# First mixer, weight units 10 to 36: the low part formed by an accumulating transfer (raw added to minus high) instead of by VectorE's subtraction

## The reference

```
def first_block(x, mem, ...):
    h = rmsnorm(x, norm_mix_g[i])
    c_q, c_kv, k_r, u_ssm, x_q, gate_logits = split_combined(h @ w_in[i])
    y_a = mla_branch(c_q, c_kv, k_r, ...) @ w_o_mla[i]       # causal attention, 8 heads
    y_b = s5_branch(u_ssm, ...) @ w_o_ssm[i]                 # complex linear scan over the tokens
    y_c = cross_branch(x_q, mem, ...) @ w_o_cross[i]         # attention to 256 memory rows
    gates = jax.nn.sigmoid(gate_logits + b_gate[i]).reshape(bsz, l, N_BRANCH, D_MODEL)
    merged = gates[:, :, 0] * y_a + gates[:, :, 1] * y_b + gates[:, :, 2] * y_c
    x = x + merged @ w_out[i]
    ...                                                      # feed-forward part with a convolution
```

## Time and profile before

| | |
|---|---|
| median of 3 runs | 1732.19 us (1731.37 to 1732.69) |
| span of the profiled execution | 1730.6 us |
| PE busy | 95% of the span |
| DVE busy | 62% |
| ACT busy | 42% |
| POOL busy | 11% |
| data moved by DMA | 284.23 MB, 164 GB/s in the mean |

### The profile page before, as it was taken

The page is one execution under the profiler, slowest core; times in us unless marked ns, Lnnn a source line. Parts: engine busy times, 40 slices in busy tenths (PEclk is TensorE's granted clock), DMA queues, the critical chain, the costliest instruction groups (busy, mean ns, idle before and its releaser), DMA issues.

```text
span 1730.6 us, 28437 instructions
## 1 busy us (share of the span) xinstructions
PE 1639.9 (95%) x11368; PEld 1516.5 (88%) x11368; DVE 1080.5 (62%) x1271; ACT 731.1 (42%) x771; POOL 198.5 (11%) x188
## 2 busy tenths in 40 slices
PE   6888788989999999999999999989999999999998
PEld 5876677889998999988998999989998999989997
DVE  6779996777777555555456655555555555665555
ACT  6344225454545333345434433343333553443332
POOL 4935570000000000001000000000000020000000
PEclk9989899999999999999999999989999999999999
DMA  6412323355553554544344554545554444545552
GB/s 243 147 73 98 107 95 140 124 210 187 190 188 127 195 195 177 187 151 166 147 170 146 199 195 173 191 148 174 191 188 151 186 153 149 174 180 186 182 191 97
DMA packets 39613, 284.23 MB, mean 164 GB/s; under 512 B 4513, under 2 KB 4513, under 8 KB 5729
## 3 DMA queue, kind: packets, MB, share of 16 engines
q1 hardware_dynamic: 38864, 278.93, 44.6%
q0 software_dynamic: 384, 2.98, 0.5%
q10 hardware_dynamic: 272, 1.05, 0.2%
HBM read 281.89 MB, written 1.05 MB: 163 GB/s over the span
## 4 chain that ended last, share of the span: by engine, by line
PE 82%; DVE 9%; POOL 4%; issue 3%; ACT 2%; DMA 0%; DVEq 0%; ACTq 0%; POOLq 0%
PE p L614 19%; PE p L615 19%; PE p L616 19%; PE big L614 7%; PE big L615 7%; PE big L616 7%; DVE ar L1523 2%; DVE wlo L510 2%; DVE ar L1784 1%; POOL sm L525 1%; POOL ar L544 1%; ACT whi L502 1%; DVE ar L1531 1%; POOL ar L548 0%; PE p L786 0%
## 5 line engine op out<-in xcount | busy, mean ns | idle before, releaser
L510 DVE TENSOR_TENSOR wlo<-raw,whi 128x2048 fp32r<-128x2048 f32 x256 | 591.3, 2312 | 338.8 <-ACT whi L502 337.2
L614 PE MATMUL p<-h_hi,whi 128*128 128x256 f32 x2568 | 735.1, 286 | 6.8 <-DVE h_lo L1531 5.9
L615 PE MATMUL p<-h_lo,whi 128*128 128x256 f32 x2568 | 731.0, 285 | 0.0
L616 PE MATMUL p<-h_hi,wlo 128*128 128x256 f32 x2568 | 730.6, 285 | 0.0
L502 ACT ACTIVATE whi<-raw 128x2048 fp32r<-128x2048 f32 x256 | 488.9, 1914 | 320.1 <-PE big L616 163.7
L614 PEld LDWEIGHTS p<-h_hi,whi 128*128 128x128 f32 x2568 | 497.4, 194 | 18.2 <-issue 9.2
L615 PEld LDWEIGHTS p<-h_lo,whi 128*128 128x128 f32 x2568 | 497.5, 194 | 1.8
L616 PEld LDWEIGHTS p<-h_hi,wlo 128*128 128x128 f32 x2568 | 497.1, 194 | 0.0
L614 PE MATMUL big<-whi,b_hi 128*128 128x512 f32 x454 | 177.9, 392 | 1.0 <-DVE b_lo L1523 1.0
L615 PE MATMUL big<-wlo,b_hi 128*128 128x512 f32 x454 | 177.5, 391 | 0.0
L616 PE MATMUL big<-whi,b_lo 128*128 128x512 f32 x454 | 176.6, 389 | 0.0
(11 more groups left out here) (238 smaller groups left out, 1606.9 us busy)
## 6 DMA issues: line engine op xcount, KB each, us to landing
raw<-weights SPq DMA_DIRECT2D x263, 1024.0 KB, 4.8
ar<-consts POOLq DMA_DIRECT2D x1, 2112.0 KB, 8.3
ar<-mem ACTq DMA_DIRECT2D x1, 1024.0 KB, 6.6
x_rows<-x SPq DMA_DIRECT2D x1, 1024.0 KB, 10.2
out<-ar SPq DMA_DIRECT2D x2, 512.0 KB, 2.7
ar<-ssm_bc SPq DMA_DIRECT2D x1, 512.0 KB, 14.7
ar<-g_final POOLq DMA_DIRECT2D x1, 512.0 KB, 4.0
c<-consts SPq DMA_DIRECT2D x1, 504.5 KB, 4.2
```

The source lines that it names most:

```text
L510: dve.tensor_tensor(wlo[:, r, :], raw[:, r, :], whi[:, r, :].bitcast(F32), ALU.subtract)\
L614: pe.matmul(out, s[0], m[0], start=start, stop=False)
L615: pe.matmul(out, s[0], m[1], start=False, stop=False)
L616: return pe.matmul(out, s[1], m[0], start=False, stop=stop)
```

## The change

For units 10 to 36 DVE's subtraction is gone. ACT writes `wlo` too, right behind `whi`, as the raw weights rounded in the same way and negated (so minus high). POOL then issues a transfer that reads the unit from memory once more and adds it to `wlo` in place. The PE waits for that transfer's own semaphore, one per slot of the ring (`lo_in0` to `lo_in2`). SP's load of the next raw unit waits for `split_done`, which ACT counts up for these units when minus high is written, and DVE for all others.

```
+LO_BY_DMA = range(10, U_MIX1)
...
-                    sp.wait_ge(S("lo_done"), i * RING + (r + 1))
+                    sp.wait_ge(S("split_done"), i * RING + (r + 1))
                     sp.dma_start(raw[:, r, :], ws[i * RING + (RING + r)]).then_inc(S(f"raw_in{r}"), 16)
...
             act.activation(whi[:, r, :], raw[:, r, :], ACT.Copy).then_inc(S("hi_done"), 1)
+            if l is None and us in LO_BY_DMA:
+                if us == LO_BY_DMA[0]:
+
+                    act.wait_ge(S("split_done"), us)
+                act.activation(wlo[:, r, :], raw[:, r, :], ACT.Copy, scale=-1.0).then_inc(S("split_done"), 1)
 
         def split_dve(dve, s, l=None, m=None):
-            r = (ustat(s, l) + RING) % RING
+            us = ustat(s, l) + RING
+            if l is None and us in LO_BY_DMA:
+                return
+            r = us % RING
...
+            def add_raw(u):
+
+                r = u % RING
+                pool.wait_ge(S("split_done"), u + 1)
+                nc.gpsimd.dma_start(wlo[:, r, :], ws[u], accum_op=ALU.add).then_inc(S(f"lo_in{r}"), 16)
+
...
             for j in range(ST):
                 rotate_out(j)
+                add_raw(j + 10)
                 if j == 3:
                     rsqrt(rc, msc, 4, "big_read", plan.use("cs") + 1, "c_rstd")
                 if j == 11:
                     rsqrt(rq_, mq, 16, "mq_msq", 1, "mq_rstd")
                     rsqrt(rk_, mk, 16, "mk_msq", 1, "mk_rstd")
+            for u in range(ST + 10, U_MIX1):
+                add_raw(u)
             norm(2)
...
             def unit_in(k, l=None, extra=0):
 
-                pe.wait_ge(S("lo_done"), extra + unit(k, l) + 1)
+                if l is None and k in LO_BY_DMA:
+                    pe.wait_ge(S(f"lo_in{k % RING}"), 16 * len(range(LO_BY_DMA[0] + (k - LO_BY_DMA[0]) % RING, k + 1, RING)))
+                    return
+                pe.wait_ge(S("split_done"), extra + unit(k, l) + 1)
```

More of the change, by code:

```diff
@@ L477, in _ @@
                 for r in range(RING):
-                    sp.wait_ge(S("lo_done"), i * RING + (r + 1))
+                    sp.wait_ge(S("split_done"), i * RING + (r + 1))
                     sp.dma_start(raw[:, r, :], ws[i * RING + (RING + r)]).then_inc(S(f"raw_in{r}"), 16)
             for u in range(RING + turns * RING, U_ALL):
-                sp.wait_ge(S("lo_done"), u - RING + 1)
+                sp.wait_ge(S("split_done"), u - RING + 1)
                 sp.dma_start(raw[:, u % RING, :], ws[u]).then_inc(S(f"raw_in{u % RING}"), 16)
@@ L510, in split_dve @@
             dve.tensor_tensor(wlo[:, r, :], raw[:, r, :], whi[:, r, :].bitcast(F32), ALU.subtract)\
-               .then_inc(S("lo_done"), 1)
+               .then_inc(S("split_done"), 1)
         @block.gpsimd
@@ L1730, in first_split @@
                 dve.wait_ge(S("hi_done"), r + 1)
-                low(wlo[:, r, :], raw[:, r, :], whi[:, r, :]).then_inc(S("lo_done"), 1)
+                low(wlo[:, r, :], raw[:, r, :], whi[:, r, :]).then_inc(S("split_done"), 1)
             dve.wait_ge(S("mem_in"), 16)
```

## The result

| | before | after |
|---|---|---|
| median of 4 runs | 1732.1 us (1731.37 to 1732.69) | 1761.8 us (1755.35 to 1768.15) |
| recorded ratio | | 1.0168, 95% interval 1.0152 to 1.0184 |
| span of the profiled execution | 1730.6 us | 1753.7 us |
| mean granted clock of it | 0.976 | 0.971 |

The change makes the kernel slower by 29.7 us in the median.

The account below looks back on a forecast made before the run. DVE was taken to bound the scan's stretch. With +28.5 us there and +9 in the tail, +37.5 on 1732.2 gave 1770 us; the forecast's own range was 1750 to 1795, the wider one 1735 to 1860.

Parts of the forecast that it names:

- L: Time from a transfer's issue on POOL to its landing, taken as 8.1 us; bounds 4.8 and 11.4.
- The path S + R + L: Scan: from unit j + 8's start to unit j + 10's takes at least one PE slot, the rotation and the transfer's landing.
- The steps: Units 10 to 24: seven steps of two slots, 148.0 us against 145.5 before; with the added terms +28.5 us.
- Clock, +12: Scan's stretch: the PE's 4.5 us wait in each of seven steps lowers its clock, losing 1.7 us each time.
- Rotation, 7 x 4.4: Scan's stretch: each of seven steps includes a POOL rotation of 4.4 us before the transfer.
- Sharing, +10: Scan's stretch: raw loads beside the adds share the DMA engines, 1.5 us for each step; bounds 0 and 23 in all.
- Instructions behind rotation 11, +3: On POOL, two instructions of 6.9 us delay rotation 12 and its transfer; 3.6 us of slot cover the rest.
- The tail, +9: Units 25 to 36: +7 for the longer way through ACT and transfer, +3 for the clock, -1 for the attention's chain.
- ACT's pass: 27 more passes on ACT of 1.91 us each, 17 of them fitting in the scan's stretch.
- One pass: Rival: the add costs nothing beside copying, landing in 4.8 us; about -16 us, 1716 us; chance 0.08 for 1710 to 1728.
- covered: Rival: landing takes 5.5 to 7 us and waits are too short to lower the clock; 1735 to 1752 us, chance 0.13.
- dearer: Rival: the add costs more than two passes, 11.4 us giving 1803 us; chance 0.20 for 1795 to 1860, 0.05 beyond.

Follow-up runs that it names:

- Plain: The changed kernel with its transfer as a plain load overwriting `wlo` with the raw weights instead of adding to it: 1728.8 us, ratio 0.9973 to the kernel before.
- no_add_scan: Against the changed kernel, units 10 to 25 have no transfer, ACT writing scaled raw weights as low part; later units keep DVE's subtraction: 1710.4 us, ratio 0.9877.

## Why the prediction was right, and where its sizes were off

The forecast was 1770 us, the result 1761.8: the side, the mechanism and the likeliest case are right. The forecast loss of 37.5 us was 7.8 too high in the median and 14.4 against the profiled execution.

**L, right.** Taken as 8.1 us, measured 8.6 in the median and 7.9 to 8.7 for the seven transfers on the chain between 99 and 275 us. Plain fits an L made of two passes, as assumed: about 2.3 us fixed and twice 2.8, for my 1.5 and twice 3.3. The Trainium skill's rule for a ReduceScatter ("Collectives: The Full Stack", section "The bandwidth ceiling: the fold count and why AG ≠ RS ≠ AR"), an add costs its two source reads at half the rate, agrees with this: 5.4 against 2.8 us of the engines' time for each unit. The Trainium skill's line for this queue ("DMA: Bandwidth & Descriptors", section "Anatomy of one DMA — SWDGE (gpsimd) path"), 2.0 us plus bytes over 436 GB/s, gives 4.4 us for the plain unit and 6.8 for the added one as an estimate; the shortest measured are 5.1 and 7.9.

**The path S + R + L, right.** Units 12, 14, 16, 18, 20, 22 and 24 each started within 0.1 us after their transfer had landed. The chain of the profile first runs through the same path of the odd units (13, 15, 17) and from unit 18 on through 20, 22 and 24. From 13 to 18 the PE waited for a transfer at every unit, and then at every second, as forecast. The step from unit 10 to 12 ran over DVE and an attention product, which ended with the transfer. The rotations are released by L819, and placing the transfer ahead of the rotation (early) takes the path away and 33 us with it.

**The steps.** From unit 10 by pairs to unit 24 the working, with its clock, sharing and the instructions behind rotation 11, gives 30.7, 23.2, 21.8, 23.7, 23.7, 26.7 and 23.7, together 173.5 us. Measured: 30.3, 22.2, 21.8, 22.3, 23.5, 23.9, 23.5, together 167.4. That is 22 us more than before, where 28 were forecast, and the unit-10 start was 0.7 us earlier rather than 1 later. The terms inside it are less right than their sum, which is luck in part: the clock cost more than forecast, the sharing nothing.

- *Clock, +12: too small.* The seven slots, from the start of unit 10, 12 and so on to the rotation that each slot's output releases, took 17.2, 9.6, 9.1, 9.7, 10.7, 10.8 and 10.8 us, together 78.0, where the sum had 60.5 at full clock. The PE was busy in nearly all of it, at mean clocks of 0.70 to 0.82 (10.8 us at 0.72 is 7.8 at full clock), so some 17 us were lost, in the last three slots 2.7 to 2.9 each where I had put 1.7. (The 9.3 us above are less because the kernel before lost time to the clock too.)
- *Rotation, 7 x 4.4: nearly right.* From a rotation's start to the issue behind it 4.5 to 4.7 us went by, 1.8 us more in all, as the 0.3 us between the two were not in the sum.
- *Sharing, +10: the step that failed.* I let each transfer on the path take 1.5 us longer for the raw load beside it. The transfers on the chain took 7.9 to 8.7 us, 8.2 in the mean, so 0.1 where 1.5 was put. It is not that the raw loads stayed away. Beside the transfer of unit 18 one was issued 2.2 us ahead of it and landed 2.7 us after its issue, and the DMA engines were busy all the time (share 1.06), yet it landed in 7.9 us:

```profile
196.00:203.80 7.80, 4.04 (x25) 2.81 (x23) 6.37 (x12) 5.16 (x6) 4.37 (x5) 0.93 1.06 257
```

  In the tail, where a raw load was issued 0.1 us ahead of each add, both took longer: the adds 10.5 to 13.5 us, the raw loads 5.7 to 13.4 instead of 4.7 at the shortest. How the two must overlap in time for this to cost was not tested.
- *Instructions behind rotation 11, +3: nothing.* In POOL's timeline:

```profile
227.88 6.41 POOL L534 TENSOR_TENSOR sm<-sm 128x16 f32<-128x16 f32 x2
238.26 1.31 POOL L584 TENSOR_TENSOR s5x<-ar 128x512 f32<-128x512 f32 x1 [3.97 <-PE p L819]
```

  They end at 234.3, and POOL then idles 4.0 us for the PE. I had covered them with 3.6 us of slot only, but in the new rhythm the output that releases rotation 12 comes a whole wait later.

**The tail, +9, measured +3.4** (112.5 against 109.1). From 33 to 36 I had 21.1 us against 16.4. Measured were 22.3:

```profile
353.12 0.47 PE L632 MATMUL big<-whi,h_hi 128*128 128x512 f32 x1 [1.98 <-DMA wlo<-weights]
...
375.40 0.47 PE L632 MATMUL big<-whi,h_hi 128*128 128x512 f32 x1 [1.08 <-DMA wlo<-weights]
```

The transfers of the tail landed after 11.9 us in the median (10.5 to 13.5), for the 11.4 that I had. From 30 to 33 it was +2.0 for +2.5. What I undervalued lies before that: units 24 to 30 took 55.6 us against 60.3, -4.7 where I had -1. I put it down to DVE's relief, which no run shows by itself. The clock (+3) cost nothing: it was 1.00 from 290 to 375 us, and 0.97 over the whole tail as before.

**ACT's pass, right:** 27 of 1905 ns, and no cost seen in the stretch (no_add_scan, within the bound given there). **After the mixer:** 1366.3 us from unit 37 to the end against 1368.0, unchanged to 2 us.

**Between the profiled execution and the median** lies the clock. Span times mean clock, an estimate of the time at full clock, is 1703, 1700, 1705 and 1704 us in the four executions of the changed kernel, with spans from 1753.7 to 1766.5, and 1689 in the profiled one before. By this estimate 11 to 16 us of the loss is time at full clock and is nearly the same each time, and the rest, 9 to 20 us, comes and goes with the clock. Where in the other three the clock was lower was not recorded.

**The rivals.** One pass, covered and dearer fall by L. Plain, with an L of 5.2 us in the scan's stretch, shows what the rivals' sums were worth. It is 3.6 us faster than before, so below the bound of 5.5 us the change does gain, as forecast. But the one-pass sum was too low, 125 us for the stretch at 4.8 where plain took 146.9: the clock did not stay up there, 0.90 in the mean of the stretch. That "an early place" could have made the same transfers worth having was not among my cases: I treated the position behind the rotation as given, and it was the change's one expensive choice.

**Open:** when a raw load beside an add makes it longer; what DVE's relief is worth in units 10 to 12 and 24 to 30; how much of the clock's part filler work can win back.

## What to carry to other kernels

An instruction that others wait for takes its place in its engine's order as part of its price. Before it is put behind another, ask who releases that other one: here the PE released the rotation, the rotation let the transfer go, and the PE waited for the transfer, a loop of 22 to 24 us where two slots of work take 16. The same transfers one rotation ahead took 2.5 us longer to land in the median, and the kernel was 33 us shorter; a transfer 2.9 us shorter in the old place gave as much. And replace an engine's work by a transfer only where that engine was the bound: in the scan's stretch the relief was worth 17 us, in the last units of the mixer it cost 6.

## What the runs showed of the hardware

- An accumulating transfer of 1 MB from memory into on-chip memory, issued by POOL, with a change of type from f32 to fp32r, took 7.9 us at the shortest and 5.4 us of the 16 engines' time; the same without the add 5.1 and 2.8; a raw load of SP lands in 4.7 and takes 2.9. Where a raw load was issued 0.1 us ahead of it (the changed kernel's tail) it landed after 10.5 to 13.5 us, and those raw loads after 5.7 to 13.4.
- Its issue holds POOL for 0.89 us, that of the plain one for 0.59.
- After a wait of 5.2 us the PE ran the next unit at a mean clock of 0.65. Executions of one kernel that differ by 13 us in span agree within 5 us once the span is multiplied by its mean clock.
